# Filling three of the four residual banks with ACT copies instead of identity matmuls, in a two-layer transformer trunk with mixture-of-experts

## What is computed

```python
for layer in range(DEPTH):
    h = _rmsnorm(x, mix_norm[layer])
    if layer % 2 == 0:
        x = x + _mixer_ab(h, ...)      # 16 heads: dilated window and banded attention
    else:
        x = x + _mixer_c(h, ...)       # 16 heads: dense attention with rotary positions
    h = _rmsnorm(x, ffn_norm[layer])
    x = x + _hier_moe(h, ...)          # top group of 4, top 2 of its 8 experts, SwiGLU
```

## Time and profile before

| | |
|---|---|
| time, median of 3 executions | 683.51 us (681.3 to 683.67) |
| the profiled execution | 681.96 us |
| its span, first to last instruction | 680.1 us |
| PE busy | 588.0 us (86%) |
| ACT busy | 131.6 us (19%) |
| DVE busy | 215.1 us (32%) |
| mean granted clock of PE | 0.945 of 2.4 GHz |

### The profile page before, as it was taken

How to read it: one execution, slowest core, us unless ns; L and a number is a source line. 1 busy time by engine, 2 the same in 40 slices (tenths; PEclk the granted TensorE clock), 3 DMA queues, 4 the chain that set the end, 5 groups by cost and what they waited for, 6 DMA issues and landing times.

```text
span 680.1 us, 11635 instructions
## 1 busy us (share of the span) xinstructions
PE 588.0 (86%) x4806; PEld 418.7 (62%) x4806; DVE 215.1 (32%) x730; ACT 131.6 (19%) x343; POOL 6.6 (1%) x25
## 2 busy tenths in 40 slices
PE   9998989998999678487779899999899967948776
PEld 8786867785666355253548776678566635625353
DVE  4234354253323212020223688315332321202021
ACT  2143334241000000000021355424000000000001
POOL 0100000000000000000001000000000000000000
PEclk9998999979999987987989999998999998889789
DMA  8999821097999999999999990009799999999994
GB/s 334 421 416 419 337 93 62 7 419 285 422 421 421 419 419 420 420 422 422 418 420 421 421 386 13 1 1 384 321 422 422 422 420 418 420 421 422 422 419 163
DMA packets 35339, 233.55 MB, mean 343 GB/s; under 512 B 3920, under 2 KB 4048, under 8 KB 7888
## 3 DMA queue, kind: packets, MB, share of 16 engines
q1 hardware_dynamic: 32400, 227.49, 81.0%
q10 hardware_dynamic: 2880, 5.24, 2.2%
HBM read 231.67 MB, written 1.05 MB: 342 GB/s over the span
## 4 chain that ended last, share of the span: by engine, by line
PE 56%; DMA 25%; DVE 6%; SPq 5%; ACT 4%; issue 3%; POOL 0%; ACTq 0%; DVEq 0%; POOLq 0%
PE banks L850 12%; PE banks L682 9%; DMA ring<-in_moe_w_down 8%; DMA ring<-in_moe_w_up 8%; PE banks L770 7%; PE banks L835 6%; PE banks L869 6%; PE banks L879 5%; SPq L565 5%; DMA xT<-in_moe_w_down 4%; DMA shared<-in_rope 4%; PE banks L718 2%; PE banks L734 2%; PE banks L778 2%; PE banks L745 1%
## 5 line engine op out<-in xcount | busy, mean ns | idle before, releaser
L850 PE MATMUL banks<-ring,heads 128*32 128x256 f32 x1664 | 124.0, 403 | 13.8 <-DMA ring<-in_moe_w_up 13.8
L869 PE MATMUL banks<-ring,desk 128*32 128x512 f32 x464 | 72.2, 717 | 33.0 <-DMA ring<-in_moe_w_down 20.5
L850 PEld LDWEIGHTS banks<-ring,heads 128*32 128x32 f32 x1664 | 66.9, 116 | 52.8 <-issue 21.6
L682 PE MATMUL banks<-ring,hT 128*128 128x256 f32 x384 | 88.7, 387 | 0.0
L682 PEld LDWEIGHTS banks<-ring,hT 128*128 128x128 f32 x384 | 72.5, 193 | 12.8 <-issue 3.5
L835 PE MATMUL banks<-desk,hT 128*128 128x128 f32 x512 | 63.6, 285 | 11.9 <-issue 10.2
L835 PEld LDWEIGHTS banks<-desk,hT 128*128 128x128 f32 x512 | 62.8, 201 | 13.6 <-issue 10.9
L869 PEld LDWEIGHTS banks<-ring,desk 128*32 128x32 f32 x464 | 19.2, 127 | 74.5 <-issue 68.8
L770 PE MATMUL banks<-heads,ring 128*128 128x256 f32 x256 | 61.7, 386 | 1.9 <-ACT heads L1008 1.9
L879 PE MATMUL banks<-desk,heads 128*128 128x256 f32 x256 | 59.5, 386 | 0.0
L879 PEld LDWEIGHTS banks<-desk,heads 128*128 128x128 f32 x256 | 47.3, 190 | 19.7 <-issue 13.9
(11 more groups left out here) (149 smaller groups left out, 549.6 us busy)
## 6 DMA issues: line engine op xcount, KB each, us to landing
ring<-in_moe_w_gate SPq DMA_DIRECT2D x58, 1024.0 KB, 26.0
ring<-in_moe_w_down SPq DMA_DIRECT2D x58, 1024.0 KB, 27.0
ring<-in_moe_w_up SPq DMA_DIRECT2D x46, 1024.0 KB, 26.8
shared<-in_moe_w_up SPq DMA_DIRECT2D x18, 1024.0 KB, 25.0
ring<-in_ab_w_in SPq DMA_DIRECT2D x8, 1024.0 KB, 18.3
shared<-in_moe_w_gate SPq DMA_DIRECT2D x6, 1024.0 KB, 22.6
xT<-in_moe_w_down SPq DMA_DIRECT2D x6, 1024.0 KB, 27.4
ring<-in_c_w_in SPq DMA_DIRECT2D x6, 1024.0 KB, 26.8
```

The costliest lines, as they stand in the source:

```text
L682: ins = pe.matmul(bank2(SLAB_BANK[layer][s], NT)[:, t, :], hT[:, c, t * P:(t + 1) * P], w[:, c, :], start=(c == 0), stop=(c == NC - 1))
L850: ins = pe.matmul(bank((4, 0)[stage])[j * SLOTS:(j + 1) * SLOTS, 0:DFF], gathered[:, c, j * SLOTS:(j + 1) * SLOTS], w[:, c, :], start=(c = ...
L869: ins = pe.matmul(bank(2 + half)[j * SLOTS:(j + 1) * SLOTS, :], hiddenT[:, k, j * SLOTS:(j + 1) * SLOTS], w[:, k, half * HALF:(half + 1) * ...
```

## The change

Six of the eight identity matmuls go: pairs 0, 1 and 3 of both layers. In their place ACT copies `xT` into the bank at its own step `residual` in the list, behind the wait that the matmul had, and counts `residual_in_banks` up. The first `project` into such a bank waits for that count. Pair 2 (bank 5) keeps its matmul.

So that the projection adds to what ACT wrote, instead of overwriting it, the slabs and the scores, which used these banks last, set `start` only with the first matmul of the bank. The number of their matmuls and their order stay.

```diff
@@ -680,7 +681,7 @@
                     ins = pe.matmul(bank2(SLAB_BANK[layer][s], NT)[:, t, :], hT[:, c, t * P:(t + 1) * P], w[:, c, :],
-                                    start=(c == 0), stop=(c == NC - 1))
+                                    start=(c == 0 and t == 0), stop=(c == NC - 1), skip_group_check=True)
@@ -716,7 +717,7 @@
                         ins = pe.matmul(bank2(r, NT)[:, t, :], heads[rows, i, t * P:(t + 1) * P], keysT[rows, kt, :],
-                                        start=True, stop=True)
+                                        start=(t == 0), stop=True, skip_group_check=True)
@@ -748,14 +749,9 @@
             def residual(layer, cp):
 
-                if cp < 2:
-                    slab_taken(pe, layer, max(s for s in range(SLABS[layer]) if SLAB_BANK[layer][s] == Y[cp]))
-                elif cp == 2:
-                    pe.wait_ge(s_hT, turns_before(layer, SLABS[layer]))
-                elif layer == 0:
-                    pe.wait_ge(s_sc, NT * HEADS)
-                else:
-                    pe.wait_ge(s_p, HEADS * (layer + 1))
+                if cp != 2:
+                    return
+                pe.wait_ge(s_hT, turns_before(layer, SLABS[layer]))
                 if layer == 0:
                     pe.wait_ge(s_x[cp], 16)
                 pe.matmul(bank(Y[cp]), ident, xT[:, 2 * cp:2 * cp + 2, :].rearrange("p c t -> p (c t)"),
@@ -763,6 +759,8 @@
             def project(layer, cp, k):
                 n = first_unit(layer, "out") + k // 2
+                if k == 0 and cp != 2:
+                    pe.wait_ge(s_res, 3 * layer + (1, 2, 0, 3)[cp])
                 pe.wait_ge(s_att, PAIRS * layer + k + 1)
@@ -1007,6 +1005,17 @@
+            def residual(layer, cp):
+
+                if cp < 2:
+                    slab_taken(act, layer, max(s for s in range(SLABS[layer]) if SLAB_BANK[layer][s] == Y[cp]))
+                elif layer == 0:
+                    act.wait_ge(s_sc, NT * HEADS)
+                else:
+                    act.wait_ge(s_p, HEADS * (layer + 1))
+                A.activation(bank(Y[cp]), xT[:, 2 * cp:2 * cp + 2, :].rearrange("p c t -> p (c t)"), ACT.Copy)\
+                    .then_inc(s_res, 1)
+
@@ -1083,6 +1092,8 @@
                         take_att(layer, i)
+                    elif what == "residual" and i != 2:
+                        residual(layer, i)
```

More of the change, by code:

```diff
@@ L288, in hybrid_moe_kernel @@
         s_att = sem("attT_ready")
+        s_res = sem("residual_in_banks")
         s_proj = sem("residual_in_psum")
```

## The result

The changed kernel took 688.49 us in the median (686.03 to 688.91), the kernel before 683.49. The ratio is 1.0062, 95% interval 1.0037 to 1.0086: slower, by 2.5 to 5.9 us. The forecast was 687.3, with a range from 684.3 to 689.8.

A forecast was written before the change was run, and what follows sets the result against it. Expert-weight loads bound the kernel except in two attention holes, which set their restart. Layer 0 -0.95, layer 1 +3.0 and clock +1.7 gave +3.8 us (rounded): median 687.3 us, range 684.3 to 689.8.

The forecast's parts named there:

- Layer 0, residual 0: Layer 0's first copy, behind ACT's attT copy: an equally long wait replaces the matmul, cost +0.1 us.
- Layer 0, residual 1: Layer 0's copy behind ACT's square: projection 0.5 us earlier on PE, about 0.2 us of gain left behind DVE.
- Layer 0, residual 3: Layer 0's copy falls into ACT's 7.14 us idle time, done before PE asks: -0.86 us, likewise in layer 1.
- Layer 1, residuals 0 and 1: Layer 1's copy 0 stands behind the exponentials of scores 2 on ACT; PE waits, scores 3 come +3.9 us later.
- No slack takes it up: Behind layer 1's scores 3, DVE and ACT hold no slack for the +3.9 us; absorption was a rival, chance 0.11.
- The clock: In layer 1, PE's 5.3 us idle lowers its clock and slows the work behind the wait: +1.7 us.
- The sum: Whole kernel: -0.95 for layer 0, +3.0 for layer 1 and +1.7 for the clock make +3.8 us (rounded).
- The rival "faster": Layer 1's copy of residual 0 is done before PE asks: -3.5 us in all, 680.0 us, chance 0.04.
- The copy's direction: ACT's copies from SBUF into PSUM: 0.58 us each, bounds 0.39 to 0.8; faster PSUM access would only shave a little.

The follow-up runs named there:

- Experiment 3: The changed kernel with 18 unread identity matmuls on PE before its wait for layer 1's first copy; ratio 1.0045 to the kernel before.
- experiment 6: The changed kernel with ACT copies kept only for residuals 0 and 1 of layer 1, at their same place; ratio 1.0102 to the kernel before.
- Experiment 2: The changed kernel with layer 1's copies 0 and 1 put ahead of the exponentials of scores 2 in ACT's order; ratio 0.9980 to the kernel before.
- 4: The changed kernel with residuals 0 and 1 of layer 1 as identity matmuls on PE again; ratio 0.9983 to the kernel before.
- 10: The changed kernel's start flags alone, with all eight identity matmuls in place and no copy; ratio 1.0006 to the kernel before.
- experiment 7: Experiment 2 with layer 0's residual 0 copy also put early, ahead of the copy of attT 3; ratio 0.9952 to the kernel before.
- experiment 9: The version of experiment 7 measured again; ratio 0.9950 to the kernel before.

## Why the prediction was right

The direction, the place and the mechanism hold step by step. The median of 688.49 us is 1.2 above the forecast's 687.3, inside the range, but just outside the 686.3 to 688.3 that the forecast gave itself.

- **Layer 0, residual 0** was put at +0.1. Values to scores 4 grew from 7.46 to 7.65 us: +0.2, since the stream of projections behind the wait also ran 1.99 instead of 1.89 us.
- **Layer 0, residual 1** was put at -0.5 on PE, -0.2 behind DVE. From the square to the projection 1.60 us became 1.26, -0.34, since the copy starts 0.61 us behind the square's start and not 0.47. Up to DVE's maxima 4.59 became 4.36, -0.23. PE's scores came 0.24 earlier too, and the maxima now start 0.61 us behind the start of DVE's multiplication, the step that multiplication takes elsewhere (85.04 to 85.65 before). So both engines allowed just this much, and the missed 0.15 cost nothing.
- **Layer 0, residual 3** -0.86, and the same in layer 1 (C: 44.96 to 44.10), both as forecast. Layer 0 in all -0.89 against -0.95.
- **Layer 1, residuals 0 and 1** was put at +3.9 with the clock held. Experiment 3 measured +4.09. Of the 0.19 that were missing, 0.11 are the first projection: the values follow it by 1.06 us (413.03 to 414.09) and not by the 0.95 of a projection that had a matmul right ahead of it.
- **No slack takes it up.** Scores 3 to scores 4 is 6.92 us before and after.
- **The clock** was put at +1.7 by one row. The two groups of rows took 1.85 us more: the term was undersized by 0.15. Doubling the work behind the wait, which the forecast named as +1.9 and did not take, was the better reading here; in experiment 6 either was too little by over 2 us.
- **The sum** was +3.8. By the stretches it is +4.19, and by the ratio +4.2. The three small misses (0.06, 0.19, 0.15) add up. That the two profiled spans differ by about as much, 4.0 us, is luck: there the slower down projection stands in for the earlier start and the faster router.
- **The rival "faster"** was priced wrongly. Experiment 2 met its condition, the copies done before PE asks (but for 0.22 us), and gained 1.75 us and not 3.5: the two matmuls in front are worth nothing, because PE then waits for DVE.
- **The copy's direction.** By the Trainium skill (ScalarE: Activation LUTs, "ACT is a hardware spline evaluator") ACT reaches PSUM faster than SBUF. The copies took 0.596 us in the median, and the same shape out of PSUM into SBUF 0.597 us in the median (line 1004 before), so these runs show no difference in that length; the sources differ as well, so it isn't a clean test of the page.

Shown by experiments: the copies' place in ACT's queue as the cause (2, 4, 6), the clock's share and that it doesn't fall when PE is kept at work through the wait (3), that the flags cost nothing (10). Read from rows alone: that the two differences outside the change (router, last down projection) are the clock's. Over 141.00 to 146.00 of the kernel before, in its router, it was at 0.67, over 672.00 to 677.00 of the changed one, in its last down projection, at 0.57. Why it falls in one execution and not in the next stays open.

## What to carry to other kernels

Moving work to an idle engine moves it into that engine's queue. Before the move, look up what stands ahead of it in that queue and whether that is itself waiting: ACT was busy 19% of the time, and still PE waited 5.3 us for the copy, which stood behind exponentials that it had nothing to do with. An instruction whose inputs are long ready belongs ahead of the next wait of its queue, not at the place where its consumer's step happens to be written. And price a stall of some 5 us on TensorE twice, once for the wait and once for the work behind it at the lower clock: in these profiles the second bill was 1.85 to 4.2 us.

## What was not expected of the hardware

The same wait of 5.3 us ended in different bills of the clock: 1.85 us in two executions of the changed kernel (B of 13.34 and 13.33) and 4.2 in one of the kernel of experiment 6 (1.78 more in B, 0.55 in C). And in experiment 7 the clock fell behind waits of only 1.33 and 0.26 us at the transposes, which cost 1.65 us in C (45.75 against 44.10), and C came out the same in experiment 9. In experiment 2, with the same rows at the same distances, it held at 1.00 and C was 44.11. So a version of this kernel that takes work from TensorE can, in some executions, lose a part of the gain again to the clock.
